# Draining the value banks before the next weight split, and moving the large tiles of later stages to one SBUF alignment

## The reference

```python
h = rmsnorm(x, norm_mix)
qa, ka, va, qb, kb, vb = split(h @ w_in)            # 768 + 1536 columns
ya = swa_gqa_sinks(rope(qa), rope(ka), va) @ w_o_a  # window of 2 chunks of 64
yb = chunk_relbias_attention(qb, kb, vb) @ w_o_b    # own chunk + 8 before it
gates = sigmoid(h @ w_branch_gate + b)
x = x + (gates[0] * ya + gates[1] * yb) @ w_out
h2 = rmsnorm(x, norm_ffn)
x = x + moe(h2)      # 32 experts, two per token: (silu(h2 @ w_eg) * (h2 @ w_eu)) @ w_ed
return rmsnorm(x, norm_final)
```

## Time and profile before

| | |
|---|---|
| median of 3 runs | 2596.25 us |
| profiled execution, its own time | 2592.82 us |
| its span, first to last instruction | 2590.9 us |
| TensorE busy with matmuls | 2336.4 us, 90% of the span |
| VectorE, ScalarE, GpSimd busy | 1297.8, 1024.0, 848.0 us |
| mean granted clock of TensorE | 0.960 |
| DMA | 517.34 MB, 200 GB/s over the span |

### The profile page before, as it was taken

How to read it: one execution, slowest core, us unless ns; L and a number is a source line. 1 busy time by engine, 2 the same in 40 slices (tenths; PEclk the granted TensorE clock), 3 DMA queues, 4 the chain that set the end, 5 groups by cost and what they waited for, 6 DMA issues and landing times. The chain is left out here.

```text
span 2590.9 us, 36773 instructions
## 1 busy us (share of the span) xinstructions
PE 2336.4 (90%) x12238; PEld 1986.4 (77%) x12239; DVE 1297.8 (50%) x1949; ACT 1024.0 (40%) x1778; POOL 848.0 (33%) x799
## 2 busy tenths in 40 slices
PE   5999998999997888896999999379999999999990
PEld 4888887788886788885899998268888888888870
DVE  6012222211110777776433333657757757798774
ACT  6111111211111677774312221146646545666653
POOL 7365545530000111111322221134433434454451
PEclk9999999999998999998999999589999999999995
DMA  4247766632213667555544432378977979899977
GB/s 164 90 146 233 253 196 179 195 122 73 73 65 130 215 187 201 160 142 159 183 154 145 150 127 104 117 244 298 315 235 256 323 220 315 275 372 332 309 258 275
DMA packets 234881, 517.34 MB, mean 200 GB/s; under 512 B 24368, under 2 KB 90032, under 8 KB 233648
## 3 DMA queue, kind: packets, MB, share of 16 engines
q1 hardware_dynamic: 158528, 340.18, 37.9%
q0 software_dynamic: 32352, 95.18, 14.9%
q10 hardware_dynamic: 43920, 80.95, 8.7%
HBM read 384.56 MB, written 131.66 MB: 199 GB/s over the span
## 5 line engine op out<-in xcount | busy, mean ns | idle before, releaser
L400 DVE TENSOR_TENSOR pj_w_lo<-pj_w_raw,pj_w_hi 128x1024 fp32r<-128x1024 f32 x38 | 50.7, 1334 | 572.2 <-ACT pj_w_hi L289 572.2
L289 ACT ACTIVATE pj_w_hi<-pj_w_raw 128x1024 fp32r<-128x1024 f32 x38 | 40.2, 1059 | 586.9 <-PE pj_bank L464 517.6
L464 PE MATMUL pj_bank<-pj_hT_hi,pj_w_hi 128*128 128x512 f32 x960 | 258.5, 391 | 7.8 <-DVE pj_f_lo L417 5.7
L464 PE MATMUL pj_bank<-pj_hT_lo,pj_w_hi 128*128 128x512 f32 x960 | 258.2, 391 | 0.0
L464 PE MATMUL pj_bank<-pj_hT_hi,pj_w_lo 128*128 128x512 f32 x960 | 256.9, 389 | 0.0
L1948 POOL TENSOR_TENSOR ex_wd_lo<-weights_raw_d,ex_wd_hi 128x1024 fp32r<-128x1024 f32 x64 | 192.2, 3026 | 130.6 <-ACT ex_wd_hi L1976 130.6
L464 PEld LDWEIGHTS pj_bank<-pj_hT_hi,pj_w_hi 128*128 128x128 f32 x960 | 181.0, 189 | 46.0 <-issue 8.5
L464 PEld LDWEIGHTS pj_bank<-pj_hT_lo,pj_w_hi 128*128 128x128 f32 x960 | 181.3, 189 | 37.9
L464 PEld LDWEIGHTS pj_bank<-pj_hT_hi,pj_w_lo 128*128 128x128 f32 x960 | 180.7, 188 | 37.7
L2030 DVE TENSOR_TENSOR ex_wd_lo<-weights_raw_d,ex_wd_hi 128x1024 fp32r<-128x1024 f32 x64 | 164.6, 2611 | 10.9 <-ACT ex_wd_hi L1976 10.9
L1539 PE MATMUL mg_y_ps<-mg_aT_hi,mg_w_hi 128*128 128x256 f32 x512 | 148.3, 290 | 11.3 <-DVE mg_gated L1450 8.0
(11 more groups left out here) (278 smaller groups left out, 5831.5 us busy)
## 6 DMA issues: line engine op xcount, KB each, us to landing
weights_raw_g<-in_w_exp_gate_dram SPq DMA_DIRECT2D x128, 512.0 KB, 8.4
weights_raw_u<-in_w_exp_up_dram SPq DMA_DIRECT2D x128, 512.0 KB
weights_raw_d<-in_w_exp_down_dram SPq DMA_DIRECT2D x128, 512.0 KB
pj_w_raw<-in_w_feat_dram SPq DMA_DIRECT2D x38, 512.0 KB, 4.8
scratch_gates<-pj_f_hi ACTq DMA_DIRECT2D x32, 512.0 KB, 5.0
mg_g_in<-scratch_gates SPq DMA_DIRECT2D x128, 128.0 KB, 3.1
pj_x_in<-in_x_dram SPq DMA_DIRECT2D x16, 512.0 KB, 3.5
scratch_qk<-pj_f_hi ACTq DMA_DIRECT2D x16, 512.0 KB, 7.0
```

Of the source, the lines that this page charges most:

```text
L289: act.activation(w_hi[n % 2][:], w_raw[n % 2][:], ACT.Copy).then_inc(whi_done, 1)
L400: dve.tensor_tensor(w_lo[n % 2][:], w_raw[n % 2][:], w_hi[n % 2][:], ALU.subtract).then_inc(wlo_done, 1)
L464: last = pe.matmul(eight[4 * p + b][:], w[p][:, k * P:(k + 1) * P], h[:, k, b * NB:(b + 1) * NB], start=(k == 0 and n == 0), stop=(k == KD ...
```

## The change

There are two parts. In project, `evacuate_tokens(s)` is now called ahead of the split of piece n + 2 on ScalarE, and on VectorE between the scaling and the split. In the allocation, `Routes` gets a tile `fill` of 40 fp32 columns (160 bytes per partition) that nothing uses, and in experts `rows` and `targets` are allocated last.

```diff
@@ project, scalar
             for n, (s, c) in enumerate(PIECES):
+                if n == last_piece(s) and KINDS[s] == TOKENS:
+
+                    evacuate_tokens(s)
                 if n + 2 < len(PIECES):
                     split_weights(n + 2)
-                if n == last_piece(s):
-                    if KINDS[s] == TOKENS:
-                        evacuate_tokens(s)
-                    else:
-                        evacuate(s)
-                        store(s)
+                if n == last_piece(s) and KINDS[s] != TOKENS:
+                    evacuate(s)
+                    store(s)
@@ project, vector
                 if n + 2 < len(PIECES):
                     scale_weights(n + 2)
+                if n == last_piece(s) and KINDS[s] == TOKENS:
+
+                    evacuate_tokens(s)
+                if n + 2 < len(PIECES):
                     split_weights(n + 2)
                 if n == last_piece(s) and KINDS[s] == SPLIT:
                     evacuate(s)
-                if n == last_piece(s) and KINDS[s] == TOKENS:
-                    evacuate_tokens(s)
@@ Routes
+ROUTES_FILL = 40
...
         self.last = st.sb("last", [1, EXPERTS], I32)
+        self.fill = st.sb("fill", [P, ROUTES_FILL])
@@ experts
-        rows = st.sb("rows", [P, 1], U32)
-        targets = st.sb("targets", [P, 1], U32)
         x_in = st.sb("x_in", [P, D])
...
         y = st.sb("y", [P, D])
+        rows = st.sb("rows", [P, 1], U32)
+        targets = st.sb("targets", [P, 1], U32)
```

## The result

The change took the kernel from 2595.74 us (median of 4 runs, 2594.32 to 2597.88) to **2559.24 us** (median of 4, 2558.90 to 2560.51). The ratio is 0.986, with a 95% interval of 0.9843 to 0.9877. The forecast was 2564, in a range of 2557 to 2585. The profiled execution took 2560.51 us where it was 2592.82, with a span of 2558.6 where it was 2590.9. So the two traces lie 32.3 us apart, and the two medians 36.5.

The account below looks back on a forecast made before the run. TensorE, busy 90% of the span, was taken as the bound. Closing holes in project (16 us) and a faster matmul pace in experts (16 us) gave 32 us off, from a median of 2596.25 to 2564, range 2557 to 2585.

Parts of the forecast that it names:

- Part 1, what goes: Project, around the two value steps: lost time of pieces 18, 19, 22 and a hole goes, together 17.9 us.
- Part 1, what comes: Project: the split of piece 19 now stands behind all eight drains and stores; 1.5 us taken as its price.
- A wait for L400 of piece 19: Project: TensorE waits once for the low part of piece 19, 1.4 us, bounds nothing and 7.
- the sign to look for: Project: TensorE waiting once for piece 19's low part, 1 to 3 us; over 5 us would prove the prediction wrong.
- The chain behind it: Project's drain: first store near 404.2, last copy 13.5 us later, ScalarE free at 420.9, piece 19 ready at 423.1.
- Rival (b): Project: the late split becomes the wait, piece 19 starts 12 us late, the order keeps 6 us; 2574, chance 0.06.
- Rival (c): Experts: common alignment makes stationary and moving reads meet more often, 6.8 ns per matmul, 22 us slower; 2602, chance 0.03.
- Part 2, the mechanism: Experts: equal operand offsets let matmul runs settle from 233.5 to 226.7 ns; 19.1 us less 2.9, so 16 us.
- The DMA term: Experts: DMA can't feed a 3% faster pace in the busiest 100 us, which takes back 2.9 us.
- Rival (a): Experts: addresses have no say and the pace stays at 233.5 ns; 2580 us, chance 0.32.
- the two rules of the Trainium skill quoted in the prediction: TensorE never waits on anyone, and its two operands have a read port each; so relative addresses can't matter in experts.
- Rival (d): Attend and merge: padding does nothing for what it names, something else shifts by a few us; no separate chance given.

Follow-up runs that it names:

- experiment 1: Kernel after with the old tile layout, so only the new order in project: 2578.00 us, ratio 0.9941 to the kernel before.
- experiments 2 and 3: Kernel before with the new layout alone, 2574.74 us; kernel before with rows and targets allocated last and no padding, 2580.63 us.
- experiment 8: Kernel after with a 64-byte gap ahead of project's split weights, their tiles at 192 and the transposed input at 128: 2584.35 us.
- Experiment 10: Kernel after with one stationary tile of experts, xT_lo, moved by 64 bytes and all else as before: 2564.52 us.
- experiment 4: Kernel before with the padding alone, moving tiles of experts at 128 and stationary ones at 192: 2594.84 us, ratio 1.000.
- experiments 5 to 7: Kernel after with a gap of 32, 96 or 128 bytes ahead of x_in in experts, moving the stationary tiles: 2576.14, 2581.04 and 2574.72 us.

## Why the prediction was right

**The total.** 32 us were forecast, and the two traces differ by 32.3: 16.9 of project and 15.5 of experts, with the other stages cancelling to within 1 us. The medians differ by 36.5. The forecast took the profiled execution before to lie 3.4 us below its median and the one after the same; the one before lay 2.9 below (2592.82 against 2595.74), the one after 1.3 above (2560.51 against 2559.24). These 4.2 us are scatter of single executions, for which the sum had no term.

**Part 1, what goes.** 17.9 us were to go; by the same windows 9.54 + 0.09 + 5.6 + 2.26 = 17.5 went. The order alone gave 16.5 us in experiment 1.

**Part 1, what comes.** A wait for L400 of piece 19 was predicted at 1.4 us, between 0 and 7. It came at 0.83, at the place named, within these bounds but under the 1 to 3 us that were named as the sign to look for. The chain behind it was right in its total and wrong in two sizes. ScalarE was free at 418.4, not 420.9. The first store was issued at 403.55 (predicted 404.2), and the last copy came 416.16 - 403.55 = 12.6 us behind it, not 13.5. The last two issues took 2.03 us where the earlier trace rows had 3.07. Against that, the low part took 2.35 us where I had copied 1.23 from the earlier trace rows. In that time GpSimd ran this:

```profile
419.47 1.28 POOL L254 TENSOR_TENSOR pj_ro_lo<-pj_x_in,pj_ro_hi 128x512 fp32r<-128x512 f32 x1
```

It had started first and ended at 420.75, 1.26 us after VectorE's start; behind it VectorE took another 1.09. In experiment 1 the same L400 came just behind that instruction and took 1.23:

```profile
422.67 1.23 DVE L400 TENSOR_TENSOR pj_w_lo<-pj_w_raw,pj_w_hi 128x1024 fp32r<-128x1024 f32 x1 [2.07 <-ACT pj_w_hi L289]
```

The Trainium skill, "SBUF — State Buffer", section "SBUF: two separate sides", says that VectorE and GpSimd share a port pair; the trace agrees with that here. The slow case was in the trace of before too, and not among: at 411.90 the split of piece 19 took 2.05 us, with 0.98 of a GpSimd instruction left. That the two wrong sizes, 2.5 us early and 1.1 late, left a wait near the forecast is luck.

Rival (b), the late split as the bottleneck, would have needed ScalarE to be free at 431.4. Stores were faster, although the DMA share was at its full width: from issue to landing a median of 5.3 to 5.5 us, where the old drain had 7.0 to 7.8. Rival (c), a slower pace from the common offset, did not come: 228.0 ns.

**Part 2, the mechanism.** The sum took the pace from 233.5 to 226.7 ns for 62 of 72 matmuls, 19.1 us, and gave 2.9 back to DMA. The stage gained 15.5, against 16 predicted. Three sizes in it were off and nearly cancel. A tile's period can be read from the starts of its transposes, before:

```profile
1923.73 0.60 PE L2105 MATMUL ex_a_ps<-ex_idt,ex_a 128*128 128x128 f32 x4
...
1941.85 0.60 PE L2105 MATMUL ex_a_ps<-ex_idt,ex_a 128*128 128x128 f32 x4
```

and after:

```profile
1921.22 0.60 PE L2111 MATMUL ex_a_ps<-ex_idt,ex_a 128*128 128x128 f32 x4
...
1938.95 0.60 PE L2111 MATMUL ex_a_ps<-ex_idt,ex_a 128*128 128x128 f32 x4
```

18.12 us became 17.73. Between the first and the last `ex_a` transpose lie 45 periods, of which one is short (12.5 us before, 12.3 after). Together they went from 809.8 to 792.9 us, which is 16.9; 16.3 of these lie within runs (3036 distances, 5.4 ns each). That is 2.2 less than 19.1, since a run needs ten matmuls to settle and not five. The DMA term isn't there: the distance within runs is 227.8 to 228.1 ns in every tenth of the stage, the one with the busiest DMA (share 1.03) too. The stage's ends took 1.4 back: up to the first transpose it took 28.6 us before and 29.5 after, behind the last one 11.0 and 11.5. That isn't a cost of the layout: the two ends together took 39.6 us before, 41.0 in experiment 1 with the old layout, and 41.0, 39.4 and 40.8 in the change and experiments 2 and 3 with equal offsets. So 2.9 for DMA was the step that failed. The total came out because runs settle later than I had said (2.2 us) and the ends happened to be longer (1.4), and that it did is luck.

**Rival (a), 0.32.** It was the case that the two rules of the Trainium skill quoted in the prediction make. Experiments 2, 3, 8 and 10 contradict it: the addresses of tiles that its matmuls read move TensorE's pace by 7 ns. The argument for it, that the slow pace is also seen at equal alignment, was true but is the start of a run. The argument against it, that 48 matmuls in a row never settle, was the one that decided.

**Rival (d).** Attend came out 1.9 shorter and merge 2.5 longer, within the 3 us that I had allowed. Among the kernels run here attend lay between 354.4 and 359.3 us and merge between 437.4 and 439.9, under either layout, so neither is an effect of the padding. (The five kernels whose project took over 820 us have attend at 358.9 to 359.3, the others at 354.4 to 359.1; why it is often shorter there wasn't looked into.) It did nothing for them, as experiment 4 shows directly.

**What is shown and what isn't.** Shown: the two parts' sizes and their independence, the place of the new wait, and that the pace hangs on the difference of two start addresses modulo 256 (0 and 256 fast; 32, 64, 96 and 128 slow; 192 tried only in the value pieces of experiment 8, where one matmul of three stayed fast). Not shown: why. Experiment 10 puts the larger cost on the matmul whose own stationary tile is off (9.1 ns in the gate projection), and smaller ones on the matmul before it (2.2) and the one behind (1.7). That would fit reads of two tiles that get into each other's way, but nothing here looks at the reads themselves, and the fast matmul in experiment 8 isn't explained by it. Other widths than 512 columns and other types than fp32r weren't tried.

## What to carry to other kernels

When matmuls run back to back and the pace itself is the bound, compare the distance of their starts between stages of the same shape. A stage that is slower by 3% without any wait may have its stationary and moving tiles at different offsets modulo 256 bytes, and one small tile allocated ahead of the large ones is enough to do it: allocate those last, no padding needed. When banks become final one by one and another engine drains them, let it start with the first; what is queued behind the drain then needs its slack counted, and here it had all but 0.8 us of it.

## What the runs showed of the hardware

- A run of 512-column fp32r matmuls settles to 226.7 ns when the stationary and the moving tile start at the same offset modulo 256 bytes, and stays at 232 to 234 when they don't (stationary tile 32, 96 and 128 bytes further in experiments 5 to 7, 64 in the kernel before and in 1, 4 and 8). With the stationary tile 64 bytes behind instead (192 modulo 256, the value pieces of 8) the three kinds of matmul came to 230.2, 229.6 and 227.2. The common offset itself has no say (128 or 224).
- Even then, the first ten matmuls behind a run of 128-column transposes are some 4 ns slower (mean of the second to the tenth distance 231.2, the first left out). With `xT_lo` alone moved the down projection's runs settled within the first few, with no explanation.
- The low-part subtraction on VectorE (128 x 1024) took 1.23 us alone, and 2.35 and 2.05 when a GpSimd operation had started first and had 1.26 and 0.98 us left. Where GpSimd's came second (kernel before, L400 at 194.31, L254 at 194.52) VectorE took 1.23 and GpSimd 2.17 in place of 1.28.
- TensorE's granted clock fell and came back around the old holes (0.92 over pieces 18 and 22); with the holes closed it was 1.00 over pieces 17 to 23, a hole of 0.83 us included. The price of a hole is thus more than its length: 2.3 us of the gain were piece 22 alone.
